# Moving copies of the input half to ScalarE, the block sums into the first pair, and one correction split ahead of two rotations

## The reference, cut to what matters

```python
h = rms_norm(x, g_pre)                    # x: 1024 tokens x 1024 channels
proj = h @ w_in                           # 1024 x 7424
(a_b, a_c, a_x, a_z, b_q, b_k, b_v, b_z, m_q, m_z, gate_logits) = jnp.split(proj, idx, axis=-1)
ua = (short_gated_conv(a_b, a_c, a_x, w_conv) * silu(a_z)) @ w_up_a
q, k = partial_rope(b_q, pos), partial_rope(b_k, pos)
ub = (window_attention_with_sink(q, k, v, sink) * silu(b_z)) @ w_up_b
um = (memory_cross_attention(m_q, mk, mv) * silu(m_z)) @ w_up_m
merged = gates[0] * ua + gates[1] * ub + gates[2] * um
return x + rms_norm(merged @ w_out, g_post)
```

## Time and profile before

| what | value |
|---|---|
| median of 3 runs | 942.04 us (941.89 to 942.9) |
| the profiled execution, its own time | 942.66 us |
| its span | 940.8 us |
| PE busy | 915.8 us (97%) |
| PE weight loads busy | 768.4 us (82%) |
| DVE busy | 619.5 us (66%) |
| ACT busy | 422.6 us (45%) |
| POOL busy | 378.4 us (40%) |

### The profile page before, as it was taken

One profiled execution on the slowest core, in us unless ns is written; L12 is line 12 of the kernel. 1 busy time (PEld: TensorE's weight loads), 2 busy tenths in 40 slices (PEclk: granted clock), 3 DMA queues, 4 the chain that ended last, 5 costly groups with the idle time before them and its releaser, 6 DMA issues. The chain is left out here.

```text
span 940.8 us, 12512 instructions
## 1 busy us (share of the span) xinstructions
PE 915.8 (97%) x4360; PEld 768.4 (82%) x4360; DVE 619.5 (66%) x1057; ACT 422.6 (45%) x802; POOL 378.4 (40%) x260
## 2 busy tenths in 40 slices
PE   5999999999999999999999999999999999999997
PEld 4788778888888888888888888888888888888885
DVE  5799966655556666656576278888896367763443
ACT  7434465444445466544462434343443553432211
POOL 2457834444444344444434744444442644300000
PEclk9999999999999999999999999999999999999999
DMA  7242656342424333624253422222222874641222
GB/s 281 85 119 82 168 175 204 103 157 101 157 101 160 110 118 107 194 95 171 100 173 132 146 67 80 84 83 81 79 78 85 320 234 146 224 156 68 90 90 89
DMA packets 81181, 124.43 MB, mean 132 GB/s; under 512 B 7008, under 2 KB 40416, under 8 KB 81120
## 3 DMA queue, kind: packets, MB, share of 16 engines
q1 hardware_dynamic: 81120, 123.65, 39.8%
HBM read 90.46 MB, written 33.55 MB: 132 GB/s over the span
## 5 line engine op out<-in xcount | busy, mean ns | idle before, releaser
L660 POOL TENSOR_TENSOR ring<-spots,ring 128x512 fp32r<-128x512 f32 x218 | 311.9, 1434 | 401.7 <-ACT ring L1063 388.9
L733 PE MATMUL pm<-hc,ring 128*128 128x512 f32 x728 | 286.7, 394 | 2.2 <-POOL ring L660 2.2
L735 PE MATMUL pm<-hc,ring 128*128 128x512 f32 x728 | 284.1, 390 | 0.0
L734 PE MATMUL pm<-hc,ring 128*128 128x512 f32 x728 | 283.7, 390 | 0.0
L1063 ACT ACTIVATE ring<-spots 128x512 fp32r<-128x512 f32 x218 | 136.6, 628 | 260.3 <-PE pm L735 183.8
L733 PEld LDWEIGHTS pm<-hc,ring 128*128 128x128 f32 x728 | 136.8, 188 | 29.3 <-issue 2.5
L735 PEld LDWEIGHTS pm<-hc,ring 128*128 128x128 f32 x728 | 136.6, 188 | 28.9
L734 PEld LDWEIGHTS pm<-hc,ring 128*128 128x128 f32 x728 | 136.8, 188 | 26.8
L1289 ACT ACTIVATE area<-area 128x1024 f32<-128x1024 f32 x24 | 25.5, 1061 | 60.6 <-DMA area<-raw_d 60.6
L1013 PE MATMUL pm<-hc,ring 128*128 128x512 f32 x128 | 49.9, 390 | 0.0
L1014 PE MATMUL pm<-hc,ring 128*128 128x512 f32 x128 | 49.8, 389 | 0.0
(11 more groups left out here) (206 smaller groups left out, 1617.6 us busy)
## 6 DMA issues: line engine op xcount, KB each, us to landing
spots<-in_w SPq DMA_DIRECT2D x116, 256.0 KB, 3.0
raw_d<-area SPq DMA_DIRECT2D x72, 256.0 KB, 2.0
area<-raw_d SPq DMA_DIRECT2D x24, 512.0 KB, 3.5
area<-in_x SPq DMA_DIRECT2D x16, 512.0 KB, 4.8
spots<-in_wup SPq DMA_DIRECT2D x24, 256.0 KB, 3.9
q_d<-area_r SPq DMA_DIRECT2D x16, 256.0 KB, 4.4
area<-raw_d SPq DMA_DIRECT2D x16, 256.0 KB, 3.2
area<-in_wmem SPq DMA_DIRECT2D x16, 256.0 KB, 2.9
```

The costliest lines, as they stand in the source:

```text
L660: nc.gpsimd.tensor_tensor(ring[:, n % RING, 1, :], operand(n), ring[:, n % RING, 0, :].bitcast(F32), ALU.subtract).then_inc(lo_made, 1)
L733: pe.matmul(bank, hi, moving_hi(k), start=(k == 0), stop=False)
L734: pe.matmul(bank, hi, moving_lo(k), start=False, stop=False)
L735: mm = pe.matmul(bank, lo, moving_hi(k), start=False, stop=(k == HC - 1))
```

## The change

For the second half of h (blocks n = 8 to 15) the float32 copy is made by ScalarE, right behind the high part (new `copy_h` of ScalarE, releasing `h_copied_act`). VectorE keeps the low parts of the odd blocks, and waits for that copy before each. In blocks 12 to 15 VectorE now makes T1, T3 and T2 of one block each. The two low parts of T1 come behind `sum_s4` and ahead of `rotate(3)` and `rotate(4)` instead of in step P6 of pair 3.

```diff
@@ gpsimd, low_of_h
-                pool.wait_ge(h_copied, n + 1)
+                if n < KC:
+                    pool.wait_ge(h_copied, n + 1)
+                else:
+                    pool.wait_ge(h_copied_act, n - KC + 1)
@@ tensor, first_pair
-                            pe.wait_ge(h_copied, m - 3)
+                            if m - 4 < KC:
+                                pe.wait_ge(h_copied, m - 3)
+                            else:
+                                pe.wait_ge(h_copied_act, m - 3 - KC)
+                                pe.wait_ge(h_lo_dve, h_lo_count(m - 4, h_lo_dve))
@@ scalar
+            def copy_h(n):
+
+                nc.scalar.activation(f32(H_BLOCKS[n][2], HALF), spare[n % 4], ACT.Identity,
+                                     scale=gpre[:, n % KC:n % KC + 1]).then_inc(h_copied_act, 1)
...
             for n in range(2 * KC):
                 high_of_h(n)
+                if n >= KC:
+                    copy_h(n)
@@ vector, copy_h
-                dve.wait_ge(h_hi_made, n + 1)
+                if n < KC:
+                    dve.wait_ge(h_hi_made, n + 1)
+                elif n % 2:
+                    dve.wait_ge(h_copied_act, n - KC + 1)
...
-                nc.vector.tensor_scalar(f32(place, HALF), spare[n % 4], g, None, ALU.mult).then_inc(h_copied, 1)
+                if n < KC:
+                    nc.vector.tensor_scalar(f32(place, HALF), spare[n % 4], g, None, ALU.mult).then_inc(h_copied, 1)
@@ vector, sum_t1, sum_t3, sum_t2
-                dve.wait_ge(h_copied, KC + j + 1)
+                dve.wait_ge(h_copied, j + 1)
+                dve.wait_ge(h_copied_act, j + 1)
...
-                dve.wait_ge(h_copied, KC + HC + j + 1)
+                dve.wait_ge(h_copied_act, HC + j + 1)
...
-                    dve.wait_ge(h_lo_pool, KC - 1)
+                    dve.wait_ge(h_lo_pool, h_lo_count(KC + HC - 1, h_lo_pool))
@@ vector, order
                 if n >= KC + HC:
-                    sum_t1(n - KC - HC)
+                    j = n - KC - HC
+                    sum_t1(j)
+                    sum_t3(j)
+                    sum_t2(j)
             swap_rows(0)
             times_cos(0)
-            for j in range(HC):
-                sum_t3(j)
-            for j in range(HC):
-                sum_t2(j)
             rotate(0)
...
             sum_s4(P_DIRECT)
+            low_of_combination(T1)
             rotate(3)
             rotate(4)
...
                     add_p6(p)
-                    if p == P_DIRECT:
-                        low_of_combination(T1)
```

More of the change, by code:

```diff
@@ L301, in hybrid_layer @@
         inv_made, xs_act = sem("inv_made"), sem("xs_act")
-        x_turned, h_copied, comb_hi = sem("x_turned"), sem("h_copied"), sem("comb_hi")
+        x_turned, h_copied, h_copied_act, comb_hi = sem("x_turned"), sem("h_copied"), sem("h_copied_act"), sem("comb_hi")
         h_hi_made, h_lo_pool, h_lo_dve = sem("h_hi_made"), sem("h_lo_pool"), sem("h_lo_dve")
```

## The result

The changed kernel takes 947.62 us (median of 6 runs, 946.26 to 951.0) against 942.37 us of the kernel before (6 runs beside them, 941.89 to 943.99): a ratio of 1.0058, 95% interval 1.0048 to 1.0068. It is slower by 5.3 us, outside the range that was given. The profiled execution took 946.31 us with a span of 944.5 us, 3.7 us more than before; it is one of the two fastest of the six.

A forecast was written before the change was run, and what follows sets the result against it. TensorE bounds the kernel, with two reachable waits of about 2 us: first wait -1.9, second +1.6, first pair +0.1, together -0.2 us from the median 942.04, so 941.8 us, range 940.1 to 943.7 us.

The forecast's parts named there:

- the first of the part by part working: Copies to ScalarE: block 15's low part on VectorE holds TensorE 0.1 us, range 0 to 1.8 us; 1.9 us and more, 5 in 100.
- is paid in full: A TensorE stall at block 15 shifts its whole chain and costs its own length, up to 1.8 us.
- The fall of the clock: Rival: the longer wait ahead of the first scores drops TensorE to 1.2 GHz, costing 2.5 us, so 944.3 us; 5 in 100.
- the wait at the first scores: TensorE's second wait, for the low k window's load, grows by 1.6 us to 3.5 us.
- the wait at P5: TensorE's first wait, ahead of P5 of pair 3, falls from 2.16 to about 0.3 us, bounds 0 and 1.5 us.
- the first wait was VectorE's and not GpSimd's: Ahead of P5, VectorE's two low parts of T1, ending at 106.75 us, release TensorE, not GpSimd's L660.
- VectorE's freed time ends in the wait for the store: Ahead of times_cos(2), VectorE's wait for the store grows from 2.32 to some 8 to 12 us.
- the gain at P5 is given up at the first scores: Time the first wait gives back, 1.9 us, is lost at the second, except 0.3 us from earlier loads.
- which the change leaves alone: From last_queries to the first scores, 10.94 us of DMA stays as it is.
- both waits gone: Far end of the faster rival: waits at P5 and scores vanish, 4.1 us, so 938.0 us; faster by over 0.2%, 12 in 100.
- The low parts of T1 were priced at 2.3 us: On VectorE ahead of the rotations, the two low parts take 2.3 us, between 1.2 us alone and 3.18 us beside GpSimd.
- 0.3 us earlier: On GpSimd's queue: last_queries, and so the loads, come 0.3 us earlier; bounds 1.0 us earlier and 0.9 us later.

The follow-up runs named there:

- Experiment 4: The whole change, but on VectorE the sums of block 14 moved behind block 15's low part: 943.2 us, ratio 1.0010 against the kernel before.
- experiment 5: The kernel before with seven extra copies on VectorE ahead of block 15's low part, nothing of the change: 947.73 us, ratio 1.0062.
- experiment 1: Only ScalarE's copies of the second half of h, on the kernel before; sums and low parts of T1 not moved: 942.29 us, ratio 0.9999.
- experiment 6: The kernel before with five extra copies on VectorE ahead of block 15's low part: 944.04 us, ratio 1.0020.
- experiment 2: Only the low parts of T1 moved ahead of rotate(3) and rotate(4), on the kernel before: 942.71 us, ratio 1.0007.
- experiment 3: The whole change, but sums T3 and T2 back at their old place behind times_cos(0): 943.66 us, ratio 1.0009 against the kernel before.
- experiment 7: The kernel before with TensorE's first scores behind product P6 of pair 4 instead of ahead of it: 942.13 us, ratio 1.0002.
- (12): Experiment 4 with the rotation chain moved up on the queues of ScalarE, GpSimd and SP: 943.73 us, ratio 1.0018 against the kernel before.
- experiment 9: The kernel before with GpSimd's rope_low(4) ahead of the low part of weight tile 19: 943.68 us, ratio 1.0013.
- (8): The edits of experiments 2 and 7 together, on the kernel before: 943.16 us, ratio 1.0011.
- (10): Experiment 2 with GpSimd's rope_low(4) also ahead of weight tile 19: 943.68 us, ratio 1.0014 against the kernel before.
- (11): Experiment 1 with GpSimd's rope_low(4) also ahead of weight tile 19: 942.53 us, ratio 1.0004 against the kernel before.

## Why the prediction was wrong

**The step that failed** is the first of the part by part working: "I take 0.1 us, with 0 and 1.8 us kept for the range" for block 15's low part on VectorE. The mechanism was named (sums ahead of a low part that TensorE needs, collisions with GpSimd); its size was off: 2.86 us of wait where 0.1 us was taken and 1.8 us was the bound. Two premises failed. The bound was built on the three sums of block 14 alone, started at 41.5 us, when ScalarE's copy of block 14 is done. But the three sums of block 13 stand ahead of them on the same queue; these began at 40.94 us and would have ended at 42.7 us even at 0.6 us each. In fact block 14's sums started at 43.85 us, because those of blocks 12 and 13 were drawn out and late too (38.74 us row: 1.61 us; 42.75 us row: 0.54 us of idle time ahead and 1.18 us). The 0.1 us rested on "GpSimd is busy there only part of the time". It was busy from 41.66 to 46.76 us, and the first two of the three sums took 1.78 and 1.76 us. The trace of the kernel before had shown it just as busy, from 41.18 to 45.80 us:

```profile
41.18 1.67 POOL L667 TENSOR_TENSOR hc<-area,hc 128x512 fp32r<-128x512 f32 x1 [2.07 <-DVE area L1384]
42.81 2.99 POOL L660 TENSOR_TENSOR ring<-spots,ring 128x512 fp32r<-128x512 f32 x2
```

Experiment 4 takes these three sums from ahead of the low part and loses the wait; experiment 5 makes the wait without the change, and a loss of the same size with it.

**What the wait costs** was taken as itself ("is paid in full"). It cost 1.47 us more, since the clock fell to half behind it. The fall of the clock was a rival of the prediction, but tied to the wait at the first scores, with a price of 2.5 us and 5 in 100. It was wrong, too, to conclude from one execution that waits of 1.92 and 2.16 us are harmless: the clock falls behind the wait at P5 in experiment 1 (2.14 us), experiment 5 (2.16 us) and experiment 6 (2.18 us). There it is hidden, because the wait at the scores takes it up; at block 15 it was paid.

**What held.** That the first wait was VectorE's and not GpSimd's: moving the low parts of T1 shortens it, and then `take_c11` releases P5, as forecast. That ScalarE carries the copies for nothing, and that VectorE's freed time ends in the wait for the store (forecast 8 to 12 us, measured 11.41 us; the time of 71.3 to 71.9 us for `times_cos(2)` was missed by 4.4 us, with TensorE's chain about 5 us late). That the gain at P5 is given up at the first scores holds in experiments 2 and 3. It does not in the change and in experiment 4, where the wait at P5 falls by 1.2 and 0.8 us and the one at the scores grows by 0.15 and 0.35 us only: from `last_queries` to the scores it takes 10.25 and 10.43 us there, not the 10.94 us "which the change leaves alone". Why was not tested.

**What the prediction did not see.** It priced both waits gone at 4.1 us. By the chain read in experiment 7, the transposes of the first probabilities can't start before about 132.4 us, for VectorE's softmax stands behind the store `raw_d`; TensorE reached them at 132.50 us before. So the second wait could not be won by earlier loads alone.

**What was off in size.** The low parts of T1 were priced at 2.3 us, at most 3.18 us. They took 3.48 us in experiment 2 and 4.59 us in experiment 4. So `take_c11` comes 3.5 us later in experiment 2, not 2.0 us, the wait at P5 falls to 1.7 us, not 0.3 us, and `last_queries` comes 0.4 us later, not 0.3 us earlier.

**What stays open.** Experiments 2, 3 and 4 lie 0.07 to 0.10% above before. A fall of the clock behind the longer wait at the scores, where no later wait hides it, would explain it. The profiles fit: experiments 2 and 4 have the fall (943.99 and 943.2 us), experiment 3 has none (942.65 us). So do the single runs: those with a mean granted clock of 0.998 or more have medians of 942.50, 942.16 and 941.66 us in experiments 2, 3 and 4, those below it 943.89, 944.04 and 943.26 us, while for the kernel before beside them the two medians are 942.15 and 942.55 us. That is an observation, no experiment. The scatter of the changed kernel goes the same way: its two slowest runs (949.16 and 951.0 us) have clocks of 0.992 and 0.994, its two fastest (946.26 and 946.31 us) 0.997. The 0.8 us ahead of block 15 in the profiled execution of the change are no part of what was changed, as far as the traces tell: they arise at the first matmul of block 4, which starts at 26.73 us there, and at 26.00, 25.81 and 25.79 us in experiments 3, 4 and 12, which hold the same code up to that point.

## What to carry to other kernels

An engine with idle time has none to give at the place where another engine waits for its next instruction: before putting work there, list the instructions ahead of the one that is waited for, from the point where the engine last stood idle, and price all of them with the dearer row, that of the collision with the neighbour. Look in the trace whether the neighbour is busy there, and don't guess it. A work queue's order can cost more than its length: the same instructions in the order of experiment 4 cost 4 us less. And before shortening a wait, follow the next one down the chain: here a wait moved twice (from P5 to the scores, from there to the probabilities) and never went.

## What the runs showed of the hardware

- **VectorE and GpSimd hold each other up nearly instruction by instruction.** With two inputs in SBUF, a 128x512 instruction of VectorE takes 0.69 us alone and 1.76 to 1.78 us beside GpSimd, one of GpSimd 1.27 to 1.30 us alone and 1.72 us beside VectorE (changed kernel). Two low parts took 4.25 us beside 6.14 us of GpSimd (experiment 9).
- **TensorE's clock falls behind waits of 2.1 to 3.7 us in some executions and not in others.** The granted clock reads 0.50 from 48.90 to 51.60 us in the changed kernel, and seven steps took 1.47 us more. Matmuls at half clock follow waits of 2.14 us (experiment 1), 2.16 and 3.20 us (5), 2.18 us (6), 2.27 us (4), 2.70 us (the change), 2.71 us (2), 3.29 us (9) and 3.69 us (12). None follow waits of 2.07 us (the change), 2.15 us (7), 2.16 us (before), 2.44 us (8), 2.56 us (10), 2.87 us (3) and 3.23 us (11). So the length of the wait alone does not decide it. A wait of 1.60 us cost 1.8 us, so hardly more than itself.
- **The fall can come late.** In experiments 1, 2, 4 and 5 (there behind P5) the first slow matmul started 0.8 to 1.4 us after TensorE had gone on at full clock (experiment 1: on at 106.74 us, slow from 107.98 us).
